# A decoder trunk on one core: where GpSimd splits a head pair's values

## The reference, cut to what matters

```python
def stick_breaking_layer(x, norm_g, w_in, w_out):
    h = rms_norm(x, norm_g)
    q, k, v, gate = jnp.split(h @ w_in, 4, axis=-1)
    o = stick_breaking_attention(heads(q), heads(k), heads(v))
    return (jax.nn.silu(gate) * o) @ w_out

# inside the attention, z = q.k / sqrt(64), strict = key before query
log_1m = jnp.where(strict, jax.nn.log_sigmoid(-z), 0.0)
suffix = lax.cumsum(log_1m, axis=3, reverse=True) - log_1m
a = jnp.where(strict, jnp.exp(jax.nn.log_sigmoid(z) + suffix), 0.0)
out = a @ v
```

## Time and profile before

| what | value |
|---|---|
| median of 3 runs | 619.1 us (617.28 to 619.6) |
| the profiled execution | 617.12 us |
| its span, first to last instruction | 615.9 us |
| PE busy | 602.7 us, 98% of the span |
| DVE busy | 453.1 us, 74% |
| ACT busy | 375.5 us, 61% |
| POOL busy | 328.0 us, 53% |
| granted TensorE clock | full over the whole span |
| one pair in the steady part of the loop | 26.73 us |

### The profile page before, as it was taken

How to read it: one execution, slowest core, us unless ns; L and a number is a source line. 1 busy time by engine, 2 the same in 40 slices (tenths; PEclk the granted TensorE clock), 3 DMA queues, 4 the chain that set the end, 5 groups by cost and what they waited for, 6 DMA issues and landing times.

```text
span 615.9 us, 9902 instructions
## 1 busy us (share of the span) xinstructions
PE 602.7 (98%) x3204; PEld 507.9 (82%) x3204; DVE 453.1 (74%) x734; ACT 375.5 (61%) x814; POOL 328.0 (53%) x313
## 2 busy tenths in 40 slices
PE   6999999999999999999999999999999999999998
PEld 6888888788888888888888888888778888887886
DVE  2389497989889898884325899715798889999441
ACT  4652696676869677686435735424567776786320
POOL 4638446747575475743544455647465654454261
PEclk9999999999999999999999999999999999999999
DMA  7524312212121120212112242222412322212142
GB/s 257 131 86 121 95 33 64 85 34 85 35 84 51 51 68 34 88 49 69 61 50 78 73 130 82 92 81 59 130 43 85 87 68 68 62 59 68 35 156 84
DMA packets 61438, 48.83 MB, mean 79 GB/s; under 512 B 7520, under 2 KB 48608, under 8 KB 61408
## 3 DMA queue, kind: packets, MB, share of 16 engines
q1 hardware_dynamic: 60368, 48.44, 25.8%
q10 hardware_dynamic: 1040, 0.00, 0.1%
HBM read 44.24 MB, written 2.10 MB: 75 GB/s over the span
## 4 chain that ended last, share of the span: by engine, by line
PE 83%; DVE 11%; issue 3%; ACT 1%; DMA 1%; POOL 0%; DVEq 0%; SPq 0%; ACTq 0%
PE bank L642 22%; PE bank L644 21%; PE bank L643 21%; PE bank L785 4%; PE bank L799 3%; PE bank L761 2%; PE bank L977 2%; DVE small L1957 2%; PE bank L782 1%; DVE pr L1980 1%; DMA xs<-in_x 1%; DVE at_lo L2011 1%; PE bank L997 1%; PE bank L742 1%; DVE small L1962 1%
## 5 line engine op out<-in xcount | busy, mean ns | idle before, releaser
L506 POOL TENSOR_TENSOR w_lo<-w_raw,w_hi 128x512 fp32r<-128x512 f32 x80 | 107.7, 1358 | 155.1 <-ACT w_hi L1133 116.2
L642 PE MATMUL bank<-h_hi,w_hi 128*128 128x512 f32 x320 | 129.2, 404 | 0.7 <-ACT q L1386 0.7
L642 PE MATMUL bank<-w_hi,h_hi 128*128 128x512 f32 x320 | 127.4, 398 | 0.3 <-DVE h_lo L1606 0.2
L644 PE MATMUL bank<-h_hi,w_lo 128*128 128x512 f32 x320 | 125.5, 392 | 0.0
L643 PE MATMUL bank<-h_lo,w_hi 128*128 128x512 f32 x320 | 125.1, 391 | 0.0
L644 PE MATMUL bank<-w_hi,h_lo 128*128 128x512 f32 x320 | 125.1, 391 | 0.0
L643 PE MATMUL bank<-w_lo,h_hi 128*128 128x512 f32 x320 | 124.8, 390 | 0.0
L518 POOL TENSOR_TENSOR w_lo<-w_raw,w_hi 128x512 fp32r<-128x512 f32 x80 | 111.1, 1389 | 6.4
L516 POOL CAST w_hi<-w_raw 128x512 fp32r<-128x512 f32 x80 | 58.6, 732 | 80.4 <-DVE lo L1718 31.5
L1133 ACT ACTIVATE w_hi<-w_raw 128x512 fp32r<-128x512 f32 x80 | 48.9, 628 | 55.7 <-PE bank L644 55.5
L642 PEld LDWEIGHTS bank<-h_hi,w_hi 128*128 128x128 f32 x320 | 60.1, 188 | 14.5 <-ACT q L1386 1.1
(11 more groups left out here) (217 smaller groups left out, 1187.1 us busy)
## 6 DMA issues: line engine op xcount, KB each, us to landing
w_raw<-in_a_w_in SPq DMA_DIRECT2D x64, 256.0 KB, 2.8
w_raw<-in_w_kv SPq DMA_DIRECT2D x32, 256.0 KB, 3.1
w_raw<-in_b_w_in SPq DMA_DIRECT2D x32, 256.0 KB, 2.8
w_raw<-in_a_w_out SPq DMA_DIRECT2D x16, 256.0 KB, 2.6
w_raw<-in_b_w_out SPq DMA_DIRECT2D x16, 256.0 KB, 3.0
xs<-in_x SPq DMA_DIRECT2D x4, 512.0 KB, 6.2
qrot<-qs SPq DMA_DIRECT2D x32, 64.0 KB, 2.0
out_x<-xs SPq DMA_DIRECT2D x8, 256.0 KB, 2.7
```

Source lines behind the costliest of these rows:

```text
L506: nc.gpsimd.tensor_tensor(w_lo[s][:, :], w_raw[s][:, :], w_hi[s][:, :].bitcast(F32), ALU.subtract).then_inc(s_w, 1)
L642: pe.matmul(o, ahi, bhi, start=start, stop=False, skip_group_check=True)
L644: return pe.matmul(o, alo, bhi, start=False, stop=stop, skip_group_check=True)
```

## The change

In the loop over pairs 1 to 5, GpSimd's `values_a(i)` stands behind the wait for the first head's softplus remainder, ahead of the six slab splits; before, it stood ahead of that wait. No instruction is added or removed. Pairs 0, 6 and 7 stay as they are.

```diff
         with pool.Fori(1, KT - 2) as i:
             st.enter(i, 1, 1)
+            pool.wait_ge(s_sl, i * 6 + 3)
             values_a(i)
-            pool.wait_ge(s_sl, i * 6 + 3)
             for j in range(6):
                 split(G_BODY + 6 + j, i, 6)
             st.leave(KT - 3)
```

## The result

| | before | changed |
|---|---|---|
| median | 619.0 us (7 runs) | 621.96 us (7 runs, 618.99 to 622.92) |
| ratio | | 1.0056, 95% interval 1.0036 to 1.0076 |
| profiled execution, span | 617.12, 615.9 us | 620.2, 619.0 us |
| mean granted TensorE clock | 1.000 | 0.997 |

The changed kernel is 3 us slower; 2 were forecast.

A forecast was written before the change was run, and what follows sets the result against it. TensorE was taken to bound the kernel, with waits to win only in pair 1. 4 x 0.44 us for pairs 2 to 5 plus 0.34 for pair 1 gave 2.1 us, 619.2 profiled (621.2 on the median), range 617.7 to 624.8.

The forecast's parts named there:

- What bounds the kernel: TensorE is busy nearly throughout; gains lie only in pair 1's waits, while pairs 2 to 5 can only become late.
- What the change takes away: Pair 1's beginning: values no longer collide with VectorE's first-head copy and remainder, so first sums start 0.77 us earlier.
- What it adds: Pairs 2 to 5: values queue ahead of slab splits, k_lo ends later, attention's weight load 0.44 us late per pair.
- the sum of the turns: Alternating GpSimd and VectorE operations added up from s_sl to k_lo's end: 16.9 us in pair 3.
- Pair 1: Its early lead is waited away at k_lo before the attention's load; the pair ends 0.3 us later.
- the next pair's scores start from there, so the delay is not caught up and does not grow: Pairs 2 to 5: each pair's chain starts anew from TensorE, so the cost stays 0.44 us a pair.
- the sum of 2.1: Whole kernel: 4 x 0.44 for pairs 2 to 5 plus 0.34 for pair 1, in us.
- rival 1: GpSimd's second slab subtraction gets the turn before VectorE's ge; 5.4 us slower, 624.5, or about 630; chance 0.15 together.
- its own upper tail: Slow end of the main forecast, 1.2 to 3 us in all, which had chance 0.64.
- 2 (the cover is larger): Steady pairs: turns pack closer by 0.4 us, TensorE on time, pair 1 keeps its gain; 617.7 to 619; chance 0.15.
- 3 (the remainders are not held): VectorE's remainders don't wait for GpSimd; second head pays nothing, pair 1 gains 0.55 to 1.4 us; about 618; chance 0.04.

The follow-up runs named there:

- steady_only: Against the kernel before: values behind the first head's remainder in pairs 2 to 5 only, in front in pair 1; ratio 1.0031.
- no_values: Changed kernel without the four value instructions in pairs 1 to 5, order of semaphores kept; ratio 0.9987 to the kernel before.
- after_silu_late: Changed kernel with VectorE's silu product moved from ahead of q_lo to behind k_lo; 617.96 us, ratio 0.9991 to the kernel before.
- values_mid: Changed kernel with the values between the fourth and the fifth slab's split; ratio 0.9988 to the kernel before.
- after_again: The changed kernel itself measured once more, 6 runs; 619.63 to 622.69 us, ratio 1.0063 to the kernel before.
- pair1_only: Against the kernel before: values behind the first head's remainder in pair 1 only, in front in pairs 2 to 5; ratio 1.0021.
- ge_later: Changed kernel with four waits, all met long before, ahead of VectorE's gate step ge; ratio 1.0057 to the kernel before.
- ge_behind_memset: Changed kernel with a one-column VectorE memset ahead of its gate step ge in each pair; ratio 1.0053 to the kernel before.
- pair1_masks: Kernel with values behind the remainder in pair 1 alone, plus all six mask matmuls given three times in pairs 0 to 6; ratio 1.0138.

## Why the prediction was right, and where it was short

**What bounds the kernel** held in part: the waits of TensorE stood where the text had them, but the clock behind one of them moved the time as well. The text's 28.62 us for pair 1 ends at 127.62; by the first load of pair 2's scores, at 127.83, the pair takes 28.83. Nothing in the sum rests on it.

**What the change takes away**: the first sums of pair 1 start at 109.92 (forecast 109.87), the copy takes 0.41 and the remainder 0.68 there, and the waits of 0.36 and 0.52 are gone.

**What it adds**: the forecast was 0.44 us a pair; pairs 3 to 5 have 0.36 to 0.39. The steady_only run has the same waits alone, no_values has none, and after_silu_late takes them away by taking a turn from VectorE's side. With these three, the turns ahead of `k_lo` as the cause are shown. The 16.85 us between `s_sl` and the end of `k_lo`, against 16.91, support the sum of the turns as well; values_mid shows that it fails where an operation is counted on the wrong side of the deadline.

**Pair 1**: +0.34 forecast, +0.27 measured, with the wait for `k_lo` of 1.9 us that the text had over 1.5.

**The step that was short** is "the next pair's scores start from there, so the delay is not caught up and does not grow": the wait of 1.9 us was priced at its length. It has a second price, the scores of pair 2 at half the clock, 1.53 us, less the 0.38 of that pair's own wait. With 1.6 for pair 2 instead of 0.44 the sum of 2.1 becomes 3.3; with the measured 0.27 and 0.36 to 0.39 for the others it is 3.0, and the steps show 2.95. The fall appears in the profile of each of the five kernels with that long wait left open (the changed kernel, after_again, pair1_only, ge_later, ge_behind_memset), in none of those whose wait there is 1.6 us or less, and not when the wait is filled. The mean clocks say the same: two falls in one execution occur in 17 of the 43 executions of these five kernels, and in none of any other kernel, the 102 of the kernel before among them. That the fall follows from TensorE standing still there is shown by pair1_masks as far as one profile can.

By this term the time lies above 0.5%, to which the forecast gave 0.15, for rival 1 and its own upper tail. Rival 1 did not happen. The measured 3.0 is at the edge of the forecast's 1.2 to 3 us, and its range up to 624.8 was drawn for rival 1. That the time lies inside both is partly luck: nothing in the working stood for the missing 1 us. The direct part fits: the changed kernel's two executions without a fall (one in each set) took 618.99 and 619.63 us, 2.0 and 2.6 above 617.0, about which the quickest of before lie.

The Trainium skill's page "TensorE: Matmul & The Clock Gate" (Part 1: The HAM clock gate) says that TensorE's clock is passed at half rate when the array has been idle, and at full rate when it has been busy. This case's windows agree on the two levels and on the order (TensorE stands still for 1.8 us, then the clock is at 0.50 of its full rate for 3.4 us). The question should have been asked of the 1.9 us wait that the prediction itself found.

**Rivals.** 1 did not happen: `ge` got its turn in every pair of the profiles with the changed order; what it would cost was not measured. 2 (the cover is larger) did not hold for the changed kernel: the turns were right within 0.06 us. 3 (the remainders are not held) is refuted by the profile after, where the three `weights_lo(1)` parts take 3.63 us; alone they would take about 1.6, an estimate from the three parts of `soft`, which take 1.61 in the same pair of both kernels.

**Open.** Which executions fall at the end of the kernel. The low clock behind the last wait of 1.5 us appears in the profiles of steady_only, pair1_only and values_mid and in no other, and it costs 1.6 us (48.9 against 47.3 from the end of that wait to the end of the span). Falls do not come with the change alone: 34 of the 102 executions of the kernel before have a mean clock of 0.997 too, though at which place is not known, as none of them was profiled. The place of that wait in the run does not sort them: it ends at 571.77, 572.03 and 567.58 in these three, and at 571.60 and 566.84 in two of those without.

## What to carry to other kernels

Work moved out of one stage's way goes into another's queue: add up what the engine then does up to the next deadline, and where two engines take turns count every operation together with the one that it has to let pass. Ask of each operation near the deadline on which side of it it falls. A wait that TensorE did not have before can cost more than its length, because its clock may fall behind it. Here waits of 0.2 to 0.6 us never had that behind them, so several short waits may be better than their sum in one; no run compares the two. And look at the whole phase for who can leave the deadline's queue: one product moved behind `k_lo` took back the 3 us of loss, and with four slabs split earlier as well the kernel is ahead of both.

## What the runs showed of the hardware

* When VectorE's `ge` and GpSimd's subtraction start within 0.02 us of each other, `ge` a trace ahead, `ge` takes its lone 0.68 us and the subtraction 1.8 instead of 1.29: 24 times in 24, in pairs 0 to 5 of the changed kernel's two profiles, ge_later and ge_behind_memset.
* A wait of TensorE of 1.9 us was followed by the lower clock in five profiles of five, 1.1 to 1.7 us after its end, for 3.4 us each time. Waits of 1.3 to 1.6 us in pair 1 (three profiles) and of 1.4 us at about 460 us (fourteen) were never followed by it; one of 1.5 us near the end had it in three profiles of fourteen.
* The executions of the kernel before lie in two groups, 616.5 to 617.4 us (32 of 102; the profiled one lies there too) and 618.1 to 620.0 us. Two things lead there, as far as the profiles show. One is a fall of the clock: 34 of its 70 executions have a mean clock of 0.997, none of the lower group. The other is a slow start, which the granted clock does not show. In pair1_only, matmuls of 128x512 take 0.63 us each at 14 us into the run where the kernel before takes 0.39, and everything behind is 1.8 us later. The windows there say 1.00 in both, so only the durations tell:

```profile
14.12 0.63 PE L647 MATMUL bank<-w_lo,h_hi 128*128 128x512 f32 x1
```

```profile
14.33 0.39 PE L643 MATMUL bank<-w_lo,h_hi 128*128 128x512 f32 x1
```
